# A delta-rule kernel: 64x64 inverse products held as diagonal 32x32 blocks, per-token norms and a moved store

## The chip, the cores and the metric

One core of one Trainium2 chip runs the whole program as a single launch. The metric is device time in microseconds (us). TensorE does the matmuls, VectorE, ScalarE and GpSimd the elementwise work, and the queue of SyncE issues the transfers between HBM and SBUF; products arrive in PSUM.

## What is computed

The program is one layer of a hybrid decoder on 2,048 prompt tokens and 8 groups of 8 sample tokens: a norm and a projection, a state-space half and an RWKV-7 half side by side, an output projection, a convolutional FFN and an embedding gate. The change touches the RWKV-7 half alone. For each of 8 heads of width 64 the reference runs, token by token:

```python
kk = kk / jnp.maximum(jnp.sqrt(jnp.sum(kk * kk, axis=-1, keepdims=True)), L2_EPS)
...
def step(S, inp):
    r_t, w_t, k_t, v_t, kk_t, a_t = inp
    sa = jnp.einsum('bhvk,bhk->bhv', S, -kk_t)
    S = (S * w_t[:, :, None, :] + sa[..., None] * (kk_t * a_t)[:, :, None, :]
         + v_t[..., None] * k_t[:, :, None, :])
    return S, jnp.einsum('bhvk,bhk->bhv', S, r_t)
...
mu = jnp.mean(y, axis=-1, keepdims=True)
var = jnp.mean(jnp.square(y - mu), axis=-1, keepdims=True)
y = ((y - mu) * lax.rsqrt(var + GN_EPS)).reshape(bsz, seq_len, D_RWKV) * lnx_g + lnx_b
bonus = jnp.sum(r4 * k4 * r_k, axis=-1, keepdims=True) * v4
y = (y + bonus.reshape(bsz, seq_len, D_RWKV)) * g
```

There are two norms in it: the length of kk per token and head, and the spread of y per token and head. All arithmetic is fp32.

## The kernel before

The RWKV half is the function delta_rule (L1002). It takes the prompt in 16 turns of 128 tokens (t = 0 to 15) and the 64 sample tokens as a last one. Channels lie on the partitions, two heads of 64 to a column group, four such groups j side by side on the free axis. A turn has two halves, q = 0 and 1, of 64 tokens: a chunk. Within a chunk the recurrence is written as matrices: scores between the chunk's tokens, the inverse of a unit triangular 64x64 matrix for each head, and then the state. The inverse is built in steps: the 16x16 diagonal parts by squaring (D2, D4, D8 and the sums X2, X3, X4), then the off-diagonal parts of 32 (Z32, X32t, X32), then of 64 (Z64, X64t).

The order of a half is written out by hand. STAGES (L986) names 26 products; the first 22 (INTRA) belong to the chunk itself, and the last four (RH, U, S, Y) apply the state for the chunk before and are slotted in behind stages 1, 4, 6 and 8 (STATE_AT, L1070). TensorE walks this list in order (half, L1770), and product (L1659) writes one stage: eight calls, four j by two heads, each a 64x64 stationary matrix and 64 moving columns. One fp32 call shows as two matmul instructions and two weight loads, so a product is 16 and 16. The result goes to one of three PSUM banks of that q in turn, so stage i waits until stage i-3 has been copied out.

VectorE (copy_out, L1341) copies the stages in ADD, most with a mask or an add, and ScalarE (L1528) the stages in PLAIN. One copy is 128x256. In the same in-order queues stand, at stage numbers given by NEXT, BEFORE and HATS (L1411 to L1414 on VectorE, L1552 on ScalarE, L1767 on TensorE), three other kinds of work: prepare makes the next turn's inputs (the low-rank products w and g, ss and bonus; the tanh, exp and square-root steps; the norm nrm, of which VectorE takes a maximum, L1293, and four reciprocals, L1297), hats scales them for a chunk (L1335 to L1339), and finish makes the output rows of the turn before (mean and variance by products with a block matrix, L1765 and L1750, four reciprocals at L1389, then dn, dg, db, dbonus and y, L1392 to L1407). Both norms are held as 128x512: every channel of a head carries its own copy.

GpSimd (turn, L1229) makes the token shift of the next turn: parts low and k first, once the bonus step of the turn before is done on VectorE and the rows Z have landed, then r and v. SyncE's loop runs over t:

```python
for t in range(1, NB):
    if t >= 3:
        store_rows(sp, t - 3)
    sp.wait_ge(prep_pool, at(t - 1, PREP_POOL, "z_v"))
    sp.dma_start(Zp[:], src[:, :, t * TB - 1:(t + 1) * TB]).then_inc(z_in, 16)
```

The store waits for the y step of turn t-3 on VectorE; the load of Z (L1139, 903 KB) stands behind it in the queue. VectorE, ScalarE and GpSimd run the middle turns as a loop, TensorE's turns are written out one after another.

## Time and profile before

| | us |
|---|---|
| median of 3 runs | 3874.78 (3873.79 to 3876.77) |
| the profiled execution, its own time | 3872.04 |
| its span in the trace | 3870.2 |
| projection and state space, before delta_rule | 0 to 985 |
| delta_rule: first turn's preparation | 985 to 1019.5 |
| delta_rule: 16 turns | 1019.5 to 1765 |
| delta_rule: samples and last rows | 1765 to 1846 |
| output projection, FFN, embedding | 1846 to 3870 |

Over the whole span TensorE is busy 3426.3 us (89%) with 32052 matmul instructions and as many weight loads, VectorE 2149.5 (56%), ScalarE 1110.9 (29%) and GpSimd 430.1 (11%). In the profile PE is TensorE, PEld its weight loads, DVE is VectorE, ACT is ScalarE, POOL is GpSimd and SPq is SyncE's queue. A row such as "PE rw_bank<-rw_aT,rw_bT 64*64 64x64 f32 x16" is 16 matmul instructions of a stationary 64x64 and a moving 64x64; the duration of one matmul instruction includes its way through the array, so the spacing of starts, not the duration, tells what a stream costs. Several tiles share a buffer before the change, and the name in a row is that of the buffer: rw_D is also Z, and rw_Dt also D8. The matrices that the trace calls rw_Xt are the inverse under construction.

### The profile page before, as it was taken

What the parts mean: (1) busy time and instruction counts of PE and PEld (TensorE: products, weight loads), DVE (VectorE), ACT (ScalarE), POOL (GpSimd) and SP (SyncE); (2) the same over time, 40 slices, a digit from 0 to 9 for tenths busy, and PEclk for the clock granted to TensorE, in tenths of its full rate; (3) what the DMA queues carried; (4) which work ended last, traced back from release to release, by engine and by line L of the source; (5) the groups of instructions that cost most, each with busy time, mean ns of one, the idle gap of its engine ahead of it and who ended that gap; (6) DMA issues with size and microseconds to landing.
All of it is one profiled execution on the core that took longest, in us unless ns stands there. A gap on an engine that the chain in (4) does not pass through costs nothing.

```text
span 3870.2 us, 75287 instructions
## 1 busy us (share of the span) xinstructions
PE 3426.3 (89%) x32052; PEld 3066.9 (79%) x32052; DVE 2149.5 (56%) x3866; ACT 1110.9 (29%) x2151; POOL 430.1 (11%) x427
## 2 busy tenths in 40 slices
PE   7999974089588888887699999999999999999998
PEld 4666653065477777777699999999999999999998
DVE  2111137951577777774465555666555566665565
ACT  1001021001344444442332222452222245222224
POOL 0000000000333333330300100120000021000001
PEclk9999996569799999997899999999999999999999
DMA  5010011000211111110532222432332243232223
GB/s 200 27 39 26 26 45 13 0 2 31 62 27 27 27 27 27 27 23 22 177 112 70 66 70 66 139 115 77 105 103 68 71 139 105 70 97 75 71 75 114
DMA packets 371660, 257.65 MB, mean 67 GB/s; under 512 B 29584, under 2 KB 361872, under 8 KB 371344
## 3 DMA queue, kind: packets, MB, share of 16 engines
q1 hardware_dynamic: 371360, 253.17, 21.5%
q8 instruction: 247, 4.05, 0.4%
q14 instruction: 53, 0.43, 0.0%
HBM read 217.92 MB, written 34.03 MB: 65 GB/s over the span
## 4 chain that ended last, share of the span: by engine, by line
PE 46%; DVE 3%; ACT 1%; issue 1%; DMA 1%; POOL 0%; SPq 0%; POOLq 0%; DVEq 0%; ACTq 0%
PE oe_pg L892 13%; PE oe_pd L920 13%; PE oe_pv L892 13%; PE oe_pg L953 3%; PE oe_pd L940 3%; DVE oe_w_lo L702 1%; PE oe_pv L960 1%; ACT oe_w_hi L553 0%; DVE oe_rms L733 0%; DMA oe_raw<-in_w_ple 0%; DVE oe_x L718 0%; POOL oe_ys_lo L501 0%; DMA oe_raw<-in_w_out 0%; POOL oe_acc L519 0%; PE oe_pn L881 0%
## 5 line engine op out<-in xcount | busy, mean ns | idle before, releaser
L244 PE MATMUL in_pp<-in_xn,in_w 128*128 (+1 forms) x1728 | 514.3, 460 | 3.7 <-DVE in_xn L200 3.7
L244 PEld LDWEIGHTS in_pp<-in_xn,in_w 128*128 128x128 f32 x1728 | 329.3, 191 | 188.3 <-issue 5.9
L702 DVE TENSOR_TENSOR oe_w_lo<-oe_raw,oe_w_hi 128x1024 fp32r<-128x1024 f32 (+1 forms) x294 | 379.3, 1300 | 112.1 <-ACT oe_w_hi L553 86.7
L709 DVE TENSOR_TENSOR oe_h<-oe_pd,oe_h 128x352 f32<-128x352 f32 x576 | 292.2, 521 | 193.2 <-PE oe_pd L920 140.3
L920 PE MATMUL oe_pd<-oe_f_hi,oe_w_hi 128*128 128x352 f32 x1056 | 342.7, 325 | 8.1 <-DVE oe_h L709 8.1
L892 PE MATMUL oe_pg<-oe_xs_hi,oe_w_hi 128*128 128x352 f32 x1056 | 342.0, 324 | 6.5 <-DVE oe_xs_lo L723 6.5
L920 PE MATMUL oe_pd<-oe_f_hi,oe_w_lo 128*128 128x352 f32 x1056 | 340.4, 322 | 0.0
L920 PE MATMUL oe_pd<-oe_f_lo,oe_w_hi 128*128 128x352 f32 x1056 | 340.4, 322 | 0.0
L892 PE MATMUL oe_pg<-oe_xs_lo,oe_w_hi 128*128 128x352 f32 x1056 | 340.3, 322 | 0.0
L892 PE MATMUL oe_pg<-oe_xs_hi,oe_w_lo 128*128 128x352 f32 x1056 | 340.1, 322 | 0.0
L892 PE MATMUL oe_pv<-oe_xs_lo,oe_w_hi 128*128 128x352 f32 x1056 | 339.8, 322 | 0.0
L892 PE MATMUL oe_pv<-oe_xs_hi,oe_w_hi 128*128 128x352 f32 x1056 | 339.7, 322 | 0.0
L892 PE MATMUL oe_pv<-oe_xs_hi,oe_w_lo 128*128 128x352 f32 x1056 | 339.6, 322 | 0.0
L553 ACT CAST oe_w_hi<-oe_raw 128x1024 fp32r<-128x1024 f32 (+1 forms) x294 | 312.2, 1073 | 89.2 <-DMA oe_raw<-in_w_out 36.6
L619 ACT COPY oe_gp<-oe_pg 128x352 f32<-128x352 f32 x110 | 50.0, 455 | 781.5 <-PE oe_pg L892 781.5
L772 DVE TENSOR_SCALAR oe_cv<-oe_gp,oe_cw 128x352 f32<-128x352 f32 (+1 forms) x132 | 60.3, 457 | 316.1 <-issue 167.9
L920 PEld LDWEIGHTS oe_pd<-oe_f_hi,oe_w_hi 128*128 128x128 f32 x1056 | 199.0, 188 | 12.2 <-DVE oe_h L709 9.6
L892 PEld LDWEIGHTS oe_pg<-oe_xs_hi,oe_w_hi 128*128 128x128 f32 x1056 | 198.7, 188 | 9.4 <-issue 5.5
L151 DVE COPY in_zout<-in_pp 128x352 f32<-128x352 f32 x42 | 22.0, 524 | 322.2 <-PE in_pp L244 322.2
L892 PEld LDWEIGHTS oe_pg<-oe_xs_lo,oe_w_hi 128*128 128x128 f32 x1056 | 198.9, 188 | 0.2
L920 PEld LDWEIGHTS oe_pd<-oe_f_hi,oe_w_lo 128*128 128x128 f32 x1056 | 199.0, 188 | 0.0
L892 PEld LDWEIGHTS oe_pg<-oe_xs_hi,oe_w_lo 128*128 128x128 f32 x1056 | 198.9, 188 | 0.0
(419 smaller groups left out, 7186.2 us busy)
## 6 DMA issues: line engine op xcount, KB each, us to landing
oe_raw<-in_w_gate SPq DMA_DIRECT2D x66, 512.0 KB, 4.0
oe_raw<-in_w_val SPq DMA_DIRECT2D x66, 512.0 KB, 4.0
oe_raw<-in_w_down SPq DMA_DIRECT2D x66, 512.0 KB, 3.6
oe_raw<-in_w_out SPq DMA_DIRECT2D x48, 512.0 KB, 3.7
oe_raw<-in_w_pg SPq DMA_DIRECT2D x48, 512.0 KB, 3.7
scratch_zr<-in_zout SPq DMA_DIRECT2D x12, 1232.0 KB, 4.7
rw_Z<-scratch_zr SPq DMA_DIRECT2D x15, 903.0 KB, 5.8
in_w<-in_w_in SPq DMA_DIRECT2D x6, 1536.0 KB, 16.1
```

What stands on the lines that cost most here:

```text
L151: eng.tensor_copy(dst, src).then_inc(out_sem, 1)
L244: mm = pe.matmul(pp[m % back][:, 0:TW], w[:, k, m * P:(m + 1) * P], xn[:, k, cols(n)], start=(k == 0), stop=(k == KD - 1))
L553: act.copy(w_view(kind, w[i % SLOTS][0]), w_view(kind, raw[i % 2])).then_inc(w_hi, 1)
L619: act.copy(gp[:, 2 + n * TW:2 + (n + 1) * TW], pg[b][:, 0:TW]).then_inc(gate_out, 1)
L702: dve.tensor_tensor(w_view(kind, lo), w_view(kind, raw[i % 2]), w_view(kind, hi).bitcast(F32), ALU.subtract).then_inc(w_lo, 1)
L709: dve.tensor_tensor(hm, pd[sums[key] % 3][:, 0:TW], hm, ALU.add).then_inc(h_ready, 1)
L772: end = dve.tensor_scalar(out, row(2), tap[2], tap[3], ALU.mult, ALU.add)
L892: mm = pe.matmul(out[:, 0:TW], l, r, start=(k == 0 and j == 0), stop=(k == KD - 1 and j == 2))
L920: mm = pe.matmul(pd[turn % 3][:, 0:TW], l, r, start=(q == 0 and j == 0), stop=(q == G - 1 and j == 2))
L940: mm = pe.matmul(pd[turn % 3][:, 0:TW], l, r, start=(k == 0 and j == 0), stop=(k == KD - 1 and j == 2))
L953: mm = pe.matmul(pg[m % 2][:, 0:TW], l, r, start=(k == 0 and j == 0), stop=(k == KD - 1 and j == 2))
L960: mm = pe.matmul(pv[m % 2][:, 0:TW], l, r, start=(k == 0 and j == 0), stop=(k == KP - 1 and j == 2))
```

## The change

Five things are changed, all in delta_rule.

1. The matrices of the inverse are kept as their diagonal 32x32 blocks, 128x128 in all instead of 128x256, and their products (IN_BLOCKS) are written by blocks and scores: four calls for each j, 32 columns each, one for each group of 32 partitions, so 32 instructions and 32 weight loads a product. D2 also computes the off-diagonal block of the scores (O64) in a second half of its bank, in alternation with its blocks for each j, and one ScalarE copy takes both out. X64t multiplies the blocks by 64 columns (E) and ScalarE, no longer VectorE, copies the result (XF). O64's masked copy on VectorE is gone.
2. The two norms are held by token: a sum for each head (per_head_sums) gives 128 tokens x 8, the square root, maximum and reciprocal are taken on that, and two new steps on TensorE (spread) put the values back onto 64 channels each. The eight reciprocals of 128x128 in a turn become two of 128x8.
3. The positions of several steps in the hand-written order are moved (NEXT, BEFORE).
4. SyncE stores the rows of turn t-4 instead of t-3 ahead of the load of Z.
5. At the start, two copies fill a constant part of E, and six matmuls write every PSUM bank once.

```diff
+R = C // 2
+ROWS = [slice(g * R, (g + 1) * R) for g in range(P // R)]
...
+DVE_OUT = ["Dt", "Xt", "D", "O32", "AqbT", "AakT", "X2", "X3", "X4", "X32t", "X32", "AqkT", "Sadd", "S"]
+ACT_OUT = ["D2", "Dt2", "D4", "Dt4", "D8", "Bt", "Kt", "X", "Z32", "Vt", "Z64", "XF", "RH", "U", "Y"]
+COPIED = {"AabT": ["Dt"], "Aab": ["O32"], "X64t": ["XF"], "S": ["Sadd"]}
+IN_BLOCKS = ["AabT", "Aab", "D2", "Dt2", "D4", "Dt4", "X2", "D8", "X3", "X4", "X", "Z32", "X32t", "X32", "Z64"]
...
+        for q, m in enumerate(M):
+            m["D2_O64"] = e.sb(f"D2_O64{q}", [P, 2, HP, R])
+            m["D2"], m["O64"] = m["D2_O64"][:, 0], m["D2_O64"][:, 1]
...
+        def spread(pe, out, per_head, W):
+
+            eye = masks[:, MASKS["eye"]]
+            for j in range(HP):
+                for n, h in enumerate(HALF):
+                    one = per_head[0:W, 2 * j + n:2 * j + n + 1].to_broadcast([W, HD])
+                    last = pe.matmul(v3(out, W)[h, j, :], one, eye[0:W, 0:W], start=True, stop=True)
+            return last
+
+        def per_head_sums(pe, out, rows, ones_, W):
+
+            for j in range(HP):
+                last = pe.matmul(out[0:W, 2 * j:2 * j + 2], v3(rows, W)[:, j, :], ones_, start=True, stop=True)
+            return last
...
                 for t in range(1, NB):
-                    if t >= 3:
-                        store_rows(sp, t - 3)
+                    if t >= 4:
+                        store_rows(sp, t - 4)
                     sp.wait_ge(prep_pool, at(t - 1, PREP_POOL, "z_v"))
...
+                for m in M:
+                    dve.tensor_copy(m["E"][:, :, 0:R], mask("lead")).then_inc(setup, 1)
...
-                        elif step == "nmax":
+                        elif step == "inv":
                             act_did("nrm")
-                            dve.tensor_scalar(b["nrm"], b["nrm"], L2_EPS, None, ALU.max).then_inc(prep_dve, 1)
-                        elif step in range(HP):
-
+                            dve.tensor_scalar(norm[0:W], norm[0:W], L2_EPS, None, ALU.max).then_inc(prep_dve, 1)
                             mine("nmax")
-                            dve.reciprocal(b["nrm"][:, step], b["nrm"][:, step]).then_inc(prep_dve, 1)
+                            dve.reciprocal(norm[0:W], norm[0:W]).then_inc(prep_dve, 1)
...
-                            mine("inv3")
-                            dve.tensor_tensor(b["kkn"], b["kk"], b["nrm"], ALU.mult).then_inc(prep_dve, 1)
+                            dve.wait_ge(prep_pe, at(s, PREP_PE, "spread"))
+                            dve.tensor_tensor(b["kkn"], b["kk"], v3(side[1], W), ALU.mult).then_inc(prep_dve, 1)
...
                     elif stage == "Aab":
-                        masked("D", SD if smp else MD)
-                        masked("O32", NONE if smp else MO32)
-                        masked("O64", NONE if smp else MO64)
+                        masked("D", "low8" if smp else "low16")
+                        masked("O32", "none" if smp else "cross16")
...
-                        masked(stage, SSU if smp else MSU)
-                    elif stage in ("X2", "X3", "X4", "X32t", "X64t"):
+                        masked(stage, "before8" if smp else "before")
+                    elif stage in ("X2", "X3", "X4", "X32t"):
...
-                            dve.reciprocal(sd[:, step], sd[:, step]).then_inc(post_dve, 1)
+                            dve.reciprocal(dev[0:W], dev[0:W]).then_inc(post_dve, 1)
                         elif step == "dn":
-                            mine("inv3")
-                            dve.tensor_tensor(d, d, sd, ALU.mult).then_inc(post_dve, 1)
+                            dve.wait_ge(post_pe, 3 * t + 3)
+                            dve.tensor_tensor(d, d, v3(side[0], W), ALU.mult).then_inc(post_dve, 1)
...
-                ADD = {"AabT", "Aab", "AqbT", "AakT", "X2", "AqkT", "X3", "X4", "X32t", "X32", "X64t"}
-
-                NEXT = [{3: ["kk"], 9: ["L", "t"], 15: ["nmax", 0], 16: [1], 19: ["aa", "sg"]},
-                        {3: [2, 3], 4: ["kkn", "Lp"], 7: ["b", "kp"], 19: ["bonus"]}]
-                BEFORE = [{11: ["d"]}, {8: [0, 1, 2, 3], 11: ["dn"], 13: ["dg", "db"], 14: ["dbonus", "y"]}]
+                ADD = {"AabT", "Aab", "AqbT", "AakT", "X2", "AqkT", "X3", "X4", "X32t", "X32"}
+
+                NEXT = [{3: ["kk"], 9: ["L", "t"], 12: ["inv"], 19: ["aa", "sg"]},
+                        {4: ["kkn", "Lp"], 7: ["b", "kp"], 19: ["bonus"]}]
+                BEFORE = [{13: ["d"], 19: ["inv"]}, {2: ["dn"], 13: ["dg", "db"], 14: ["dbonus", "y"]}]
                 HATS = [{13: ["bT", "aT"], 14: ["kT"]}, {15: ["bT", "aT"], 16: ["kT"]}]
-                REST = [step for i in BEFORE[1] for step in BEFORE[1][i]]
+                REST = ["dn", "dg", "db", "dbonus", "y"]
...
-                            act.activation(b["nrm"], v3(side[1], W), ACT.Sqrt).then_inc(prep_act, 1)
+                            act.activation(norm[0:W], side[1][0:W, 0:2 * HP], ACT.Sqrt).then_inc(prep_act, 1)
...
+                    elif stage == "D2":
+                        src = banks[q][at_][:, 0:2 * HP * R].rearrange("p (a j t) -> p a j t", a=2, t=R)
+                        act.copy(M[q]["D2_O64"][:], src).then_inc(act_out[q], 1)
+                    else:
+                        dst = M[q]["XF"][:] if stage == "X64t" else M[q]["E"][:, :, R:C] if stage == "Z64" else M[q][stage][:]
+                        act.copy(dst, (small if stage in IN_BLOCKS else bank)[q][at_]).then_inc(act_out[q], 1)
...
-                BEFORE = [{12: 0, 16: 1}, {}]
+                BEFORE = [{14: 0, 18: 1}, {}]
...
+                def blocks(out, l, r, j):
+
+                    for g in ROWS:
+                        last = pe.matmul(out[g, j, :], l[g, j, :], ident32[g] if r is None else r[g, j, :], start=True, stop=True)
+                    return last
+
+                def scores(out, rows, cols, j):
+
+                    for n, h in enumerate(HALF):
+                        for i in range(2):
+                            c = slice(i * R, (i + 1) * R)
+                            last = pe.matmul(out[ROWS[2 * n + i], j, :], rows[h, j, c], cols[h, j, c], start=True, stop=True)
                     return last
...
-                            pe.matmul(side[1][:, 0:HP * W], heads(), B["kk2"][:, 0:HP * W], start=True, stop=True).then_inc(prep_pe, 1)
+                            per_head_sums(pe, side[1], B["kk2"], heads()[:, 0:P:HD], W).then_inc(prep_pe, 1)
+                        elif step == "spread":
+                            dve_did("inv")
+                            if not (is_first(s) or s == 1):
+                                pe.wait_ge(post_dve, at(s - 2, POST_DVE, "d"))
+                            spread(pe, side[1], norm, W).then_inc(prep_pe, 1)
...
+                    out = (small if stage in IN_BLOCKS else bank)[q][i % NBANK]
                     for j in range(HP):
-                        for n, (l, r) in enumerate(operands):
-                            last = turned(out, l, j) if transpose else both(out, l, r, j, n == 0, n == len(operands) - 1)
+                        if stage in ("AabT", "Aab"):
+                            (l, r), = operands
+                            last = scores(out, l, r, j)
+                        elif stage == "D2":
+                            (l, r), = operands
+                            a, b = M[q]["aT"], M[q]["bT"]
+                            blocks(out, l, r, j)
+                            for n, h in enumerate(HALF):
+                                last = pe.matmul(corner[q][i % NBANK][ROWS[2 * n + 1], j, :], a[h, j, R:C], b[h, j, 0:R], start=True, stop=True)
+                        elif stage == "Z64":
+                            (l, r), = operands
+                            for n in range(2):
+                                g, g1 = ROWS[2 * n], ROWS[2 * n + 1]
+                                pe.matmul(out[g, j, :], l[g1, j, :], r[g1, j, :], start=True, stop=True)
+                                last = pe.matmul(out[g1, j, :], ident32[g1], ident32[g1], start=True, stop=True)
+                        elif stage in IN_BLOCKS or stage == "X64t":
+                            (l, r), = operands
+                            last = blocks(out, l, r, j)
+                        else:
+                            for n, (l, r) in enumerate(operands):
+                                last = turned(out, l, j) if transpose else both(out, l, r, j, n == 0, n == len(operands) - 1)
...
+                    if part == 2:
+                        pe.wait_ge(post_dve, at(t, POST_DVE, "inv"))
+                        spread(pe, side[0], dev, W).then_inc(post_pe, 1)
+                        return
...
-                        pe.matmul(side[0][:, 0:HP * W], bd64[:], ysq[:, 0:HP * W], start=True, stop=True).then_inc(post_pe, 1)
+                        per_head_sums(pe, side[0], ysq, bd64[:, 0:P:HD], W).then_inc(post_pe, 1)
...
-                NEXT = [{6: ["w"], 8: ["ss"]}, {3: ["g"], 17: ["bonus"]}]
-                BEFORE = [{11: 0, 14: 1}, {}]
+                NEXT = [{6: ["w"], 8: ["ss"], 20: ["spread"]}, {5: ["g"], 17: ["bonus"]}]
+                BEFORE = [{11: 0, 16: 1, 21: 2}, {}]
...
-                prepare(FIRST, "w", "ss", "g", "bonus")
+                for b in banks[0] + banks[1]:
+                    pe.matmul(b[:, 0:HP * C], heads(), S[0][:].rearrange("p j t -> p (j t)"), start=True, stop=True)
+                prepare(FIRST, "w", "ss", "spread", "g", "bonus")
```

## Rows read from the trace of the kernel before

**Rows 1.** All turns: us, busy (instructions) PE, PEld, DVE, ACT, POOL, clock, DMA, GB/s

```profile
1019.50:1765.00 745.50, 631.21 (x15648) 554.61 (x15650) 551.35 (x1020) 332.15 (x836) 246.96 (x258) 0.93 0.11 26
```

**Rows 2.** The same view of one turn, 1247.7 to 1294.9 us

```profile
1247.70:1294.90 47.20, 38.76 (x999) 33.77 (x997) 35.35 (x66) 21.18 (x53) 15.64 (x16) 0.97 0.10 28
```

**Rows 3.** Waits, 1019.5 to 1765 us: waiter, releaser, total us, times, longest

```profile
PE rw_bank L1606 <- DVE rw_Xt L1363: 72.6, 33, 3.8
...
PE rw_bank L1606 <- DVE rw_AakT L1348: 16.0, 12, 2.0
...
PE rw_side L1643 <- ACT rw_p_a L1481: 12.2, 13, 2.1
```

**Rows 4.** Order of time, VectorE: start, us, line, operation, count, [idle before]

```profile
1260.92 0.69 DVE L1277 TENSOR_TENSOR rw_p_kk<-rw_z,rw_k_k 128x512 f32<-128x512 f32 x1 [6.18 <-POOL rw_z L1198]
...
1274.00 1.76 DVE L1297 RECIPROCAL rw_p_kk<-rw_p_kk 128x128 f32<-128x128 f32 x2
...
1287.44 3.38 DVE L1389 RECIPROCAL rw_ysq<-rw_ysq 128x128 f32<-128x128 f32 x4
...
1291.88 0.42 DVE L1363 TENSOR_TENSOR rw_Xt<-rw_bank,rw_Xt 128x256 f32<-128x256 f32 x1 [0.19 <-PE rw_bank L1606]
...
1295.76 0.42 DVE L1339 TENSOR_TENSOR rw_kT<-rw_p_kp,rw_p_E 128x256 f32<-128x256 f32 x1
```

**Rows 5.** Order of time, SyncE's queue: the two loads of Z, a turn apart

```profile
1248.42 0.51 SPq L1139 DMA_DIRECT2D rw_Z<-scratch_zr  x1
...
1295.61 0.51 SPq L1139 DMA_DIRECT2D rw_Z<-scratch_zr  x1
```

**Rows 6.** Order of time, GpSimd: first and last token-shift step of a turn

```profile
1255.50 0.61 POOL L1194 TENSOR_TENSOR rw_z<-rw_Z 128x256 f32<-128x256 f32 x1 [12.25 <-DMA rw_Z<-scratch_zr]
...
1273.77 1.24 POOL L1198 TENSOR_TENSOR rw_z<-rw_z,rw_Z 128x512 f32<-128x512 f32 x1
```

**Rows 7.** Order of time, TensorE: products of 64x64, then one of another shape

```profile
1276.10 0.68 PE L1606 MATMUL rw_bank<-rw_Xt,rw_O 64*64 64x64 f32 x16 [2.32 <-DVE rw_Xt L1363]
...
1277.83 0.66 PE L1606 MATMUL rw_bank<-rw_aT,rw_bT 64*64 64x64 f32 x16
1278.30 0.66 PE L1606 MATMUL rw_bank<-rw_bT,rw_aT 64*64 64x64 f32 x16
...
1280.16 0.66 PE L1606 MATMUL rw_bank<-rw_D,rw_Dt 64*64 64x64 f32 x16
1280.76 1.16 PE L1620 MATMUL rw_side<-rw_p_sx,rw_g 128*128 128x128 f32 x8
```

**Rows 8.** Order of time, TensorE: instructions in two parts of its rows

```profile
1259.01 0.27 PE L1637 MATMUL rw_side<-rw_p_th,rw_w 64*128 64x128 f32 x1
1259.02 0.27 PE L1638 MATMUL rw_side<-rw_z,rw_w 64*128 64x128 f32 x1
1259.12 0.27 PE L1637 MATMUL rw_side<-rw_p_th,rw_w 64*128 64x128 f32 x1
```

**Rows 9.** Order of time, TensorE: instructions in two parts of its columns

```profile
638.96 0.63 PE L2233 MATMUL ss_bk<-ss_U,ss_RTr 128*64 128x264 f32 x4
639.41 0.63 PE L2233 MATMUL ss_bk<-ss_U,ss_RTi 128*64 128x264 f32 x4
```

**Rows 10.** Order of time, ScalarE: the exponentials, and the copy behind them

```profile
1285.76 1.28 ACT L1494 ACT_TABLE_LOAD   x1
...
1288.63 0.62 ACT L1532 COPY rw_Dt<-rw_bank 128x256 f32<-128x256 f32 x2
```

**Rows 11.** Order of time, TensorE: a gap inside the D2 product

```profile
1255.63 0.27 PE L1606 MATMUL rw_bank<-rw_D,rw_Dt 64*64 64x64 f32 x2 [0.98 <-issue]
```

**Rows 12.** Page, third part: queue, kind: packets, MB, share of 16 engines

```profile
q8 instruction: 247, 4.05, 0.4%
```

**Rows 13.** As rows 1: a stretch before the clock falls, and after

```profile
1241.30:1244.70 3.40, 0.97 (x33) 0.84 (x30) 3.21 (x6) 0.77 (x3) 1.87 (x3) 1.00 0.02 5
1244.70:1248.10 3.40, 3.40 (x69) 3.40 (x66) 3.20 (x6) 1.17 (x4) 0.00 (x0) 0.50 0.00 0
```

More of the change, by code:

```diff
@@ L988 @@
 INTRA = STAGES[:22]
-DVE_OUT = ["Dt", "Xt", "D", "O32", "O64", "AqbT", "AakT", "X2", "X3", "X4", "X32t", "X32", "AqkT", "X64t", "Sadd", "S"]
-ACT_OUT = ["D2", "Dt2", "D4", "Dt4", "D8", "Bt", "Kt", "X", "Z32", "Vt", "Z64", "RH", "U", "Y"]
-COPIED = {"AabT": "Dt", "Aab": "O64", "S": "Sadd"}
+DVE_OUT = ["Dt", "Xt", "D", "O32", "AqbT", "AakT", "X2", "X3", "X4", "X32t", "X32", "AqkT", "Sadd", "S"]
+ACT_OUT = ["D2", "Dt2", "D4", "Dt4", "D8", "Bt", "Kt", "X", "Z32", "Vt", "Z64", "XF", "RH", "U", "Y"]
+COPIED = {"AabT": ["Dt"], "Aab": ["O32"], "X64t": ["XF"], "S": ["Sadd"]}
+IN_BLOCKS = ["AabT", "Aab", "D2", "Dt2", "D4", "Dt4", "X2", "D8", "X3", "X4", "X", "Z32", "X32t", "X32", "Z64"]
 HAT_DVE = ["b", "a", "k"]
-POST_DVE = ["d", "inv0", "inv1", "inv2", "inv3", "dn", "dg", "db", "dbonus", "y"]
+POST_DVE = ["d", "inv", "dn", "dg", "db", "dbonus", "y"]
 NBANK = 3
@@ L1343, in copy_out @@
                     m, smp = M[q], is_samples(t)
[L1344 removed]
+                    src = (small if stage in IN_BLOCKS else bank)[q][STAGES.index(stage) % NBANK]
                     dve.wait_ge(mm[q], at(t, STAGES, stage))
@@ L1528, in copy_out @@
                 def copy_out(q, t, stage):
-                    dst = {"Z32": "Z", "Z64": "Z"}.get(stage, stage)
                     act.wait_ge(mm[q], at(t, STAGES, stage))
-                    act.copy(M[q][dst][:], bank[q][STAGES.index(stage) % NBANK]).then_inc(act_out[q], 1)
+                    at_ = STAGES.index(stage) % NBANK
+                    if stage == "D2" and is_samples(t):
+                        act.activation(M[q]["O64"], corner[q][at_], ACT.Copy, scale=0.0)
+                        act.copy(M[q]["D2"], small[q][at_]).then_inc(act_out[q], 1)
+                    elif stage == "D2":
[4 more added lines that the diff above has]
+                        act.copy(dst, (small if stage in IN_BLOCKS else bank)[q][at_]).then_inc(act_out[q], 1)
                 def rows_out(q, t):
@@ L1662, in product @@
                     i = STAGES.index(stage)
-                    names = [copied(n) for n in after] + ([copied(STAGES[i - NBANK])] if i >= NBANK else [])
+                    names = [c for n in [*after, *([STAGES[i - NBANK]] if i >= NBANK else [])] for c in copied(n)]
                     for sem, order in ((dve_out[q], DVE_OUT), (act_out[q], ACT_OUT)):
@@ L1687, in intra @@
                     elif stage == "D2":
-                        product(q, t, stage, [(m["Dt"], m["D"])], after=["Dt", "D"])
+                        product(q, t, stage, [(m["Dt"], m["D"])], after=["AabT", "D"])
                     elif stage == "Dt2":
@@ L1725, in intra @@
                     elif stage == "X64t":
-                        product(q, t, stage, [(m["X"], m["Z"])], after=["X32", "Z64"])
+                        product(q, t, stage, [(m["X"], m["E"])], after=["X32", "Z64"])
                 def with_state(q, t, stage):
@@ L1737, in with_state @@
                     elif stage == "U":
-                        product(q, t, stage, [(m["Xt"], m["RH"])], after=["X64t", "RH"])
+                        product(q, t, stage, [(m["XF"], m["RH"])], after=["X64t", "RH"])
                     elif stage == "S":
@@ L1813, in _ @@
                 for j in range(HP):
-                    last = both(bank[1][2], m["Xt"], m["Z"], j, True, True)
+                    last = both(bank[1][2], m["XF"], M[1]["RH"], j, True, True)
                 last.then_inc(smp_pe, 1)
@@ L1834, in _, with put @@
                 finish(SAMPLES, 1)
+                finish(SAMPLES, 2)
 def rwkv_masks():
     import numpy as np
[L1840 to L1848 removed]
+    i = np.arange(P)[:, None]
+    out = np.zeros((P, MASK_COLS), np.float32)
+    def put(name, chosen, block):
+        t = np.arange(MASKS[name].stop - MASKS[name].start)[None, :]
+        out[:, MASKS[name]] = chosen(i % block, t)
+    put("heads", lambda s, t: s // HD == t // HD, P)
+    put("eye", lambda s, t: s == t, P)
+    put("eye64", lambda s, t: s == t, C)
+    put("before", lambda s, t: s < t, C)
+    put("upto", lambda s, t: s <= t, C)
+    put("before8", lambda s, t: (s < t) & (s // DS == t // DS), C)
+    put("upto8", lambda s, t: (s <= t) & (s // DS == t // DS), C)
+    put("eye32", lambda s, t: s == t, R)
+    put("lead", lambda s, t: s == t, C)
+    put("low16", lambda s, t: (s > t) & (s // 16 == t // 16), R)
+    put("low16_t", lambda s, t: (s < t) & (s // 16 == t // 16), R)
+    put("cross16", lambda s, t: s // 16 > t // 16, R)
+    put("low8", lambda s, t: (s > t) & (s // DS == t // DS), R)
+    put("low8_t", lambda s, t: (s < t) & (s // DS == t // DS), R)
+    return out
 def sample_rows():
```

113 lines of the change are left out of this document (54 added, 59 removed).

## The prediction

> **What bounds the kernel now.** I read the busy time by stretch first: which engine fills the stage that the change touches? In the 745.5 us of the 16 turns TensorE is busy 631.21, VectorE 551.35, ScalarE 332.15 [rows 1]. None is full. A turn lasts 47.2 us, seen from one load of Z to the next [rows 5]; in one such turn TensorE is busy 38.76, VectorE 35.35 [rows 2]. So I asked next for whom TensorE waits. Over all turns it stands 72.6 us for VectorE's adds into the inverse (L1363), 16.0 for VectorE's AakT mask and 12.2 for ScalarE's tanh ahead of ss [rows 3]: 4.5, 1.0 and 0.8 us a turn. The order of time on VectorE says why the adds are late. A maximum over 128x512 and two reciprocals (1.76 us together) stand ahead of the X32t add, and TensorE's Z64 starts after 2.32 us of idling at 1276.10; four more reciprocals (3.38 us) stand ahead of the X3 add [rows 4, 7]. The AakT mask is late because VectorE idles 6.18 us for kk, which needs GpSimd's shift, which waited 12.25 us for the rows of Z [rows 4, 6]. GpSimd had read the old rows for the last time at 1273.77 + 1.24 = 1275.0, but the next load was issued only at 1295.61, behind a store that waits for y [rows 5, 6]. A turn is thus TensorE's own work plus waits for late elementwise work. The clock joins in: after a stretch in which TensorE was busy 0.97 of 3.40 us the granted clock was 0.50, and it was 1.00 before [rows 13]; that is 1.2 instead of 2.4 GHz.
>
> **TensorE's own work before.** Two 64x64 products in a row start 0.47 us apart, 16 instructions each [rows 7]: 0.029 us an instruction. The state's stages RH, S and Y count double, double and triple, so a half is 30 products, 14.0 us, and a turn 28.0. The six side products (w, ss, g, bonus, mean, variance) stream about 0.86 each: eight 128-column instructions at 0.11 [rows 8], or the same number of columns in two wide ones. That is 5.2. A change of the array's shape costs: after a 64x64 product the g product starts 0.60 later instead of 0.47 [rows 7], so 0.13; by the spacing of single instructions I take 0.10. With two changes for each of the six that is 1.2, and 0.4 for weight loads that lie bare behind them. Sum 34.8 us; 47.2 - 34.8 = 12.4 us are waits and the lower clock.
>
> **The blocks.** 24 plain block products in a turn (12 stages, two halves) go from 16 instructions of 64 columns to 32 of 32. The trace of before has no 32-row part. Its nearest rows: instructions in two parts of the rows start 0.01 us apart and each part repeats every 0.11 for 128 columns [rows 8], and two parts of the columns do the same: four instructions of 264 columns in 0.45 us [rows 9]. So parts run side by side, and a part's time goes with its columns, as 0.058 for 64 does. A block product is then eight rounds of four, each half of 0.058 plus a little, 0.032: 0.25 us. That is the low end; the high end is no parallelism at all, 32 x 0.029 = 0.93. I take 0.25, since both rows show full overlap. 24 x (0.25 - 0.47) = -5.3. The four score products save the same, -0.9. X64t stays. D2 becomes blocks and corners, 0.25 + 0.25: no change. The change of shape now comes often: 32-row stages alternate with 64-row ones, and within D2 the shape changes seven times. I count 31 changes in half 0 and 28 in half 1 against 12 a turn before: 47 x 0.10 = +4.7, the low end being 0 (where TensorE waits anyway) and the high 0.13 each, 6.1. Bare weight loads behind them: +0.9.
>
> The rows show 0.10 to 0.13 lost at a change of shape [rows 7]. The Trainium skill says under TensorEngine Tiling (Array Packing), Key Properties, that changing the tiling mode drains TensorE, and the trace agrees; without that rule the 47 changes would be free and the forecast 3741.
>
> **The norms.** ss and the variance become eight instructions with two moving columns; their 128x128 weights still load, and I take what g costs, 0.11 each: +0.1 for both. Two spreads are new, 16 instructions of 128 columns in two column parts, at 8 x 0.11 [rows 8, 9] +0.9 each, or 1.8 if the parts queue: +1.8. TensorE's own work is then 34.8 - 5.3 - 0.9 + 4.7 + 0.9 + 0.1 + 1.8 = 36.1 us. It does not shrink: the gain must come from the waits. New waits: spread waits for VectorE's reciprocal and stands in TensorE's queue ahead of X64t, but that reciprocal is due eight stages earlier; the second spread waits for one that is one short step behind the X32 add, ahead of the next half's scores. Both I take at nothing; the cover is AqkT and X64t, 0.9 us, and without it the cost is about that.
>
> **VectorE and the other queues.** Eight reciprocals (3.52 + 3.38) and the maximum of 1.26 go; two O64 masks and two X64t adds go; sixteen copies or more shrink to half. VectorE loses some 12 of its 35 us, ScalarE stays near 21. So VectorE leaves the path except in one place: from the X4 add to the X32t add it still carries dg, db, dbonus, y and three hats, 1291.88 to 1296.18 [rows 4]. TensorE has X, Z32, Vt, X32t, bonus and X32 to do meanwhile, some 2.9 us; 1.4 us of waiting stay in half 1. Half 0 has d and the hats there: 1.5. On ScalarE the exponentials with their table load take 1285.76 to 1288.63 [rows 10] ahead of the D8 copy: about 0.7 of waiting for X4. ss still waits for two sets of tanh: 0.8.
>
> **The store.** The load of Z can be issued at 1275.0 instead of 1295.6, so GpSimd starts at bonus, some 4 us before 1255.50. VectorE waits about 2 us for kk instead of 6.18, and AakT's mask no longer holds TensorE: -1.0. The store itself is an earlier turn's and has long been due; behind it only the load is queued. If the load still came late, the 1.0 would stay.
>
> **Instructions.** TensorE's instructions of all turns are fetched: 247 packets [rows 12] for 64,000 matmuls and loads, one for about 260. Inside D2 TensorE idled 0.98 us for nothing the profile names [rows 11], just while the load of 1248.42 ran. A turn before has 1,980 of them, after 3,160. I take 1.5 us a turn, between 0.5 (about as now) and 4.
>
> **The sum.** 36.1 + 1.4 + 1.5 + 0.7 + 0.8 + 1.5 (fetch) + 1.3 (clock) + 0.4 (small ones) = 43.7 us a turn. 16.5 turns x 3.5 = -58. Ahead of the first turn six matmuls of 256 columns cost 2.9 us at the full clock, 5.8 at half; the first preparation and the last rows lose reciprocals, about 3: net +2. 3872 - 58 + 2 = 3816 for an execution like the profiled one, whose 3872.04 is 2.7 below the median: 3818.
>
> **The rivals.**
> *TensorE does not pack the blocks.* If four parts cannot be fed at once, a block product costs more than 0.25. The 28 of them break the gain even at 0.25 + 3.5/28 = 0.38 us. At 0.47 a turn is 49.8: 3918. At 0.93 it is 62.7: about 4130. For it: only two parts are ever seen at once. Against: their 0.01 us between starts leaves room for four in 0.032. Chance 0.17.
> The Trainium skill, in the same page under Instruction Overhead, gives each matmul some 60 cycles however few columns it has and warns against tiling a dimension that is already small. That is this rival in its middle: by that page an estimate is 32 x 0.025 = 0.80 us, a turn of 59, 4073. Two starts 0.01 apart [rows 8] speak against it, unless the floor holds in each part.
> *Fetching binds.* With 60% more instructions and a burst of 64 in each block product, the gap of rows 11 comes at each fetch that meets the load of Z: 3 to 4 us a turn, 46: 3856. Chance 0.14.
> *The clock.* Small parts and gaps leave TensorE at 0.50 for long; if a third of its work ran so, +12 us a turn, about 4010. Against: its waits shrink. Chance 0.06.
> *Changes of shape are hidden* behind waits, or VectorE is out of the way entirely: 39 to 41 us, 3740 to 3775. Chance 0.15.
> *Nothing moves,* since TensorE's work is as long as before and other waits take the place of the old: 3867 to 3882. Chance 0.08.
>
> **How the numbers follow.** The forecast has 0.40, with a range of its own of 3790 to 3850. About 0.2% is what a measurement of this kernel can tell from no change, 7.7 us. Faster: 0.40 + 0.15 + most of the fetch case = 0.68. Same 0.08. Slower: 0.17 + 0.06 and a little = 0.24. The range takes in the hidden changes at its low end and packing at 0.45 us a product at its high end, 3740 to 3910; outside remain the worse halves of two rivals.
>
> **What would show it.** Right: block products starting 0.25 to 0.29 apart in a row and some 0.36 before a change of shape; no reciprocal over 0.2 us on VectorE; the load of Z issued right behind GpSimd's last shift step; TensorE's waits for L1363's successor down to about 3 us a turn; a turn of 43 to 44. Wrong: four blocks starting 0.03 apart each, a granted clock under 0.9 over the turns, or gaps inside products at each load of Z.

## The result, and the profile after

The changed kernel takes 3954.61 us (median of 4 runs, 3950.19 to 3967.77); the kernel before took 3874.28 beside it. The ratio is 1.021, 95% interval 1.0187 to 1.0237: 80 us slower, where 3818 was forecast with a range of 3740 to 3910. The profiled execution took 3956.61 us, its span is 3954.8. Of the four runs of the second experiment below, one is left out: it took 4163 us at a granted clock of 0.81, the other three 3926 to 3938 us.

The page's busy times first (busy, share of the span, instructions), then its row on the instruction queue (packets, MB, share of 16 engines):

```profile
PE 3496.6 (88%) x41788; PEld 3111.5 (79%) x41788; DVE 1987.6 (50%) x3700; ACT 1088.7 (28%) x2185; POOL 436.4 (11%) x427
...
q8 instruction: 323, 5.29, 0.6%
```

The instructions of all engines came in 247 packets before [rows 12], 323 now. Next a steady stretch of 500 us inside the turns (us, busy of PE, PEld, DVE, ACT, POOL, granted clock, DMA share, GB/s):

```profile
1100.00:1600.00 500.00, 421.96 (x15408) 359.63 (x15412) 249.25 (x534) 194.69 (x540) 157.27 (x156) 0.91 0.10 26
```

By VectorE's last step of y, ten turns around this stretch take 51.75 us each; before it was 47.4. VectorE is busy half the time now, 0.74 of it before [rows 1]: the reciprocals are gone, and many of its copies are half as long. For whom does TensorE wait instead? The waits of the same stretch (waiter, releaser, total us, times, longest):

```profile
PE rw_side L1127 <- ACT rw_ysq L1578: 25.2, 9, 3.0
PE rw_bank L1650 <- issue: 23.7, 26, 1.6
PE rw_bank L1639 <- issue: 10.9, 16, 1.5
PE rw_bank L1658 <- issue: 5.1, 5, 1.6
PE rw_side L1127 <- ACT rw_p_a L1506: 4.0, 8, 0.6
PE rw_bank L1644 <- issue: 3.3, 3, 1.4
PE rw_bank L1730 <- issue: 2.9, 5, 0.8
```

The waits for VectorE's adds and the AakT mask, 72.6 and 16.0 us over the turns before [rows 3], have left the list. Two kinds took their place. The first row is the variance's sum of squares (L1127); it waits for ScalarE's square, 2.6 us a turn. And all lines with "issue" together, three small ones included that are not shown, make 48.0 us, 5.0 a turn: TensorE stands still and the profile names no releaser. Before, such waits came to 4.5 us in as long a stretch.

Where the second kind sits, TensorE shows in order of time, inside D2 (start, us, line, tiles, shape, count, [idle before]):

```profile
1323.63 0.26 PE L1650 MATMUL rw_bank<-rw_D,rw_Dt 32*32 32x32 f32 x8
1323.83 0.25 PE L1730 MATMUL rw_bank<-rw_bT,rw_aT 64*32 64x32 f32 x4
1324.01 0.26 PE L1650 MATMUL rw_bank<-rw_D,rw_Dt 32*32 32x32 f32 x8
1324.20 0.21 PE L1730 MATMUL rw_bank<-rw_bT,rw_aT 64*32 64x32 f32 x1
1325.06 0.25 PE L1730 MATMUL rw_bank<-rw_bT,rw_aT 64*32 64x32 f32 x3 [0.64 <-issue]
...
1330.09 0.45 PE L1650 MATMUL rw_bank<-rw_Dt,rw_D_O 32*32 32x32 f32 x32
1330.37 0.48 PE L1650 MATMUL rw_bank<-rw_Xt,rw_D_O 32*32 32x32 f32 x32
1330.77 0.33 PE L1639 MATMUL rw_bank<-rw_rT,rw_S 64*64 64x64 f32 x4
```

One matmul of a product whose operands are all there starts at 1324.20, the other three of its four 0.86 us later. The DMA view of 1322 to 1326 us (40 slices of 0.1 us) shows what went on meanwhile:

```profile
GB/s 0 0 0 0 0 0 0 164 0 0 0 0 0 0 0 0 0 0 0 0 0 0 0 0 0 0 0 0 0 0 0 0 0 0 0 0 0 0 0 0
...
q8 instruction: 1, 0.02, 1.5%
```

A single packet, of instructions, starting at 1322.7; TensorE goes on 2.3 us behind it. No load of Z runs here. I summed, over 1020 to 1765 us, all steps of more than 0.33 us between two starts inside a product: 83.6 us in 82 places, and in 79 of them TensorE resumes 2.1 to 3.0 us after a packet's start. Before it was 7.8 us in 8 places, all 8 with the same delay. Those 8 and these 82 differ in what the packet had met: before, 7 of the packets started while a load of Z was in flight, 6.2 to 11.6 us behind the packet ahead of them; now 2 of 82 did, and half of the 82 came within 3.8 us of the packet ahead. There are 178 packets in that stretch, half of them less than 3.86 us apart and none less than 3.25. Between 1020 and 1830 us TensorE starts 48,906 matmuls and weight loads while 192 packets come in: 255 for each.

The other wait. VectorE, ScalarE and TensorE in order of time in half 0 of a turn:

```profile
1286.18 0.29 DVE L1388 TENSOR_TENSOR rw_Xt<-rw_bank,rw_Xt 128x128 f32<-128x128 f32 x1 [2.48 <-PE rw_bank L1650]
...
1287.08 0.20 DVE L1323 RECIPROCAL rw_norm<-rw_norm 128x8 f32<-128x8 f32 x1
1287.20 1.10 DVE L1361 TENSOR_TENSOR rw_bT<-rw_p_b,rw_p_E 128x256 f32<-128x256 f32 x1
1288.22 1.25 DVE L1363 SCALAR_TENSOR_TENSOR rw_aT<-rw_p_kkn,rw_p_Lp 128x256 f32<-128x256 f32 x1
1289.40 0.67 DVE L1411 TENSOR_TENSOR rw_yt<-rw_yt,rw_side 128x512 f32<-128x512 f32 x1
```

```profile
1290.10 0.63 ACT L1578 ACTIVATE rw_ysq<-rw_yt 128x512 f32<-128x512 f32 x1 [2.41 <-DVE rw_yt L1411]
```

```profile
1287.58 0.68 PE L1644 MATMUL rw_bank<-rw_masks,rw_vT 64*64 64x64 f32 x16
1290.79 1.86 PE L1127 MATMUL rw_side<-rw_bd,rw_ysq 128*128 128x2 f32 x8 [2.53 <-ACT rw_ysq L1578]
```

VectorE's d (L1411) now stands behind the hats bT and aT, which take 1.10 and 1.25 us, and ScalarE's square waits for d. The TensorE rows behind the wait are slow as well. Two stretches (columns as above) show it: TensorE is busy 0.87 of 3.40 us, and then the granted clock is 0.50, the lower level, as in [rows 13]:

```profile
1287.60:1291.00 3.40, 0.87 (x21) 0.73 (x18) 3.19 (x4) 0.99 (x4) 2.75 (x3) 0.86 0.02 5
1291.00:1294.40 3.40, 3.40 (x108) 3.20 (x109) 0.87 (x4) 0.46 (x3) 0.00 (x0) 0.50 0.78 218
```

And one turn near the end is 65.8 us long. VectorE's y there, and SyncE's queue:

```profile
1797.12 0.69 DVE L1432 TENSOR_TENSOR rw_yb<-rw_yt,rw_g_h 128x512 f32<-128x512 f32 x1 [12.53 <-DMA scratch_y<-rw_yb]
```

```profile
1783.29 10.92 SPq L1169 DMA_DIRECT2D rw_Z<-scratch_zr  x14
1794.25 3.95 SPq L1145 DMA_DIRECT2D scratch_y<-rw_yb  x2
```

y of a turn may be written once the turn before is stored. That store, NB-4's, was issued inside the loop before. Now it stands behind the 14 loads of the sample rows, and those wait for the last turn's token shift.

### The profile page after: what moved, and what is told of

Read it like the earlier page. It is cut to its first block, busy times and chain, and to the rows that moved or that the text cites. A ratio compares the mean times of both kernels' runs of the same rounds, so it can differ in the third digit from the quotient of the medians.

```text
span 3954.8 us, 94582 instructions
## 1 busy us (share of the span) xinstructions
PE 3496.6 (88%) x41788; PEld 3111.5 (79%) x41788; DVE 1987.6 (50%) x3700; ACT 1088.7 (28%) x2185; POOL 436.4 (11%) x427
## 3 DMA queue, kind: packets, MB, share of 16 engines
q8 instruction: 323, 5.29, 0.6%
## 4 chain that ended last, share of the span: by engine, by line
PE 46%; DVE 2%; ACT 1%; issue 1%; POOL 0%; SPq 0%; DMA 0%; POOLq 0%; DVEq 0%; ACTq 0%
PE oe_pg L892 13%; PE oe_pd L920 12%; PE oe_pv L892 12%; PE oe_pg L953 4%; PE oe_pd L940 4%; PE oe_pv L960 1%; DVE oe_w_lo L702 1%; DVE oe_rms L733 0%; DVE oe_x L718 0%; POOL oe_ys_lo L501 0%; PE oe_pn L881 0%; ACT oe_w_hi L553 0%; POOL oe_acc L519 0%; DMA oe_st<-in_state_conv 0%; DVE oe_h L709 0%
## 5 line engine op out<-in xcount | busy, mean ns | idle before, releaser
L892 PEld LDWEIGHTS oe_pv<-oe_xs_hi,oe_w_lo 128*128 128x128 f32 x1056 | 198.5, 188 | 0.0
```

Of the source, the lines that this page charges most:

```text
L892: mm = pe.matmul(out[:, 0:TW], l, r, start=(k == 0 and j == 0), stop=(k == KD - 1 and j == 2))
```

## The experiments

The theory: TensorE's instructions arrive too slowly for the blocks (5 us a turn), the late square adds 2.6 and the low clock behind it, and the store's new place costs some 12 us once. The rivals: the blocks' own streaming, the changes of shape, the norms' new work, or the store itself. Each result below is the median time, with its ratio to the kernel before run beside it and the 95% interval of that ratio; "the 500 us" is the stretch from 1100 to 1600 us.

**Without the blocks.** The kernel before with norms, order and store of the change:

```diff
 # kernel before, plus:
+ spread(...), per_head_sums(...)          # norms by token, as in the change
- NEXT = ... 15: ["nmax", 0], 16: [1] ... 3: [2, 3]
+ NEXT = ... 12: ["inv"] ...
- if t >= 3: store_rows(sp, t - 3)
+ if t >= 4: store_rows(sp, t - 4)
```

> The kernel before with the norms by token, the new order on the queues and the later store, but with every product of the inverse still in 64x64 parts. If the blocks' extra instructions are what lost the time (theory: TensorE waits for its instructions, some 5 us a turn), a turn has 2,000 instructions again, the gaps inside products go back to about 0.5 us a turn and the time falls below the kernel before: a turn of 44 to 45.5 us, 3820 to 3850 us, although the variance still waits 2.7 us for its square. If norms, order or store lost it, this kernel is slower than before as well: 3890 us or more.

This kernel took 3848.3 us, ratio 0.993 [0.991, 0.995]. A turn takes 45.1 us, and in the 500 us there is no wait for "issue" at all; the variance still waits 28.7 us. The blocks turn a gain into a loss.

**d ahead of the hats**, in the changed kernel:

```diff
- BEFORE = [{13: ["d"], 19: ["inv"]}, ...
+ BEFORE = [{12: ["d"], 19: ["inv"]}, ...
```

> The changed kernel with one step moved: VectorE subtracts the mean (d) after stage 12 of half 0, ahead of the hats bT and aT, instead of after stage 13 behind them. If the late square holds TensorE (theory: 2.75 to 3.2 us at the variance, once a turn, and the low clock after it), the wait falls below 0.5 us and the time by 40 to 60 us, to 3895 to 3915. If the hats that now come 0.7 us later are awaited just as long, or another step is late next, the time stays within 10 us of 3955.

It took 3928.2 us (three runs), ratio 1.015 [1.013, 1.017]: 26 us won where 40 to 60 were expected. The wait for the square fell from 25.2 to 2.4 us in the 500, so that was its cause. A turn fell from 51.75 to 49.65 us, nearly by the wait itself (2.4 us a turn). The waits for instructions stayed at 5.0 us a turn (50.2 us against 48.0), and the granted clock stayed at 0.91: the low clock that the expectation counted with the wait did not go with it.

**The store alone**, in the kernel before:

```diff
- if t >= 3: store_rows(sp, t - 3)
+ if t >= 4: store_rows(sp, t - 4)
```

> The kernel before with the store of y moved alone (four turns behind instead of three). My forecast's term: 1.0 us a turn gained, 3858 us, with VectorE's wait for kk down from 6.2 to about 2 us and the load of Z issued right behind GpSimd's last shift step. Rival: GpSimd's shift now falls beside VectorE's hats and both run slower (1.1 instead of 0.42 us each), so that nothing is won or up to 1 us a turn is lost: 3870 to 3890.

It took 3844.9 us, ratio 0.992 [0.991, 0.994]: 29 us won, more than my term. A turn falls from 47.4 to 44.9 us, and TensorE's wait for the AakT mask [rows 3] is gone from the list. The hats of half 0 were as slow in the kernel before, so the rival had no new cost to bring (see "A wait that was not listed"). One turn of 55.0 us at the end gives some back.

**Half the instructions in 24 block products**, in the changed kernel:

```diff
- for g in ROWS:
-     pe.matmul(out[g, j, :], l[g, j, :], r[g, j, :], ...)
+ if j % 2:
+     for g in ROWS:
+         pe.matmul(out[g, j - 1:j + 1, :], l[g, j, :], r[g, j - 1:j + 1, :], ...)
```

> The changed kernel with half the instructions in 24 block products a turn: each 32x32 weight block is multiplied with the 64 moving columns of two neighbouring head pairs, so the columns streamed, the shape changes, the copies and the order stay as they are, and 768 of some 3,160 TensorE instructions a turn are gone. (The product of one head of each pair is then computed with its neighbour's weights.) If instructions not yet fetched stop TensorE (theory), the gaps inside products fall from 5 to about 2 us a turn and the time by 40 to 60 us, to 3895 to 3915. If the time went to the blocks' own streaming, the shape changes or the variance, it stays within 12 us of 3955.

It took 3869.6 us, ratio 0.999 [0.998, 1.000]: 85 us less than the changed kernel, more than expected. The waits for instructions fall from 48.0 to 2.9 us in the 500. The main cause is the instructions. One thing did not stay as the expectation says: D2's blocks now stand at every second j alone, so its shape changes four times inside, not seven. How much of the 85 us this and the halved products' own streaming make is worked out further down.

**The mends.** The first mend is d ahead of the hats, as above. The second puts the store of turn NB-4 ahead of the samples' loads:

```diff
+ store_rows(sp, NB - 4)
  sp.wait_ge(prep_pool, at(NB - 1, PREP_POOL, "z_v"))
  ...
- store_rows(sp, NB - 4)
  store_rows(sp, NB - 3)
```

> The first experiment's kernel (norms by token and the later store, 64x64 products) with two mends: VectorE's d after stage 12, ahead of the hats, and the store of turn NB-4 issued ahead of the 14 loads of the samples instead of behind them. Theory: the variance's wait (38 us over the turns there) all but goes, and the one long turn at the end (55.5 instead of 45 us, y waiting for that store) is a normal one: 3848 - 33 - 10 = 3805, between 3795 and 3820. Rival: the time that d frees is lost to the hats that come later, and only the 10 us of the tail are won: 3835 to 3842.

It took 3797.9 us, ratio 0.980 [0.978, 0.982]: faster than both kernels. A turn takes 42.1 us. Its 500 us and its waits:

```profile
1100.00:1600.00 500.00, 470.59 (x12301) 426.24 (x12298) 338.23 (x698) 241.64 (x627) 201.07 (x191) 0.99 0.11 31
```

```profile
PE rw_bank L1621 <- DVE rw_Xt L1378: 11.0, 23, 0.6
PE rw_side L1118 <- ACT rw_p_a L1496: 8.1, 12, 0.7
PE rw_bank L1621 <- ACT rw_Dt L1547: 5.9, 12, 0.5
PE rw_side L1118 <- ACT rw_ysq L1560: 1.2, 8, 0.2
PE rw_bank L1621 <- issue: 0.2, 1, 0.2
```

No wait is longer than 0.7 us, and the granted clock is 0.99 where the kernel before had 0.94.

The store with the second mend, without the norms:

> The kernel before with the store moved and the store of turn NB-4 ahead of the samples' loads, nothing else. Theory: y of one turn no longer waits 9.8 us for the store behind those loads: 3845 - 10 = 3835, between 3830 and 3840. If that turn is long for another reason, 3843 to 3847.

It took 3841.4 us, ratio 0.992 [0.990, 0.994]: the long turn is 45.3 instead of 55.0 us, as expected, but the time fell by 3.5 us, not 10; the next turn is 2.1 us longer, and turns of one kernel differ by up to 2 us. The place of the loss is shown, its size in this kernel is not.

Both mends on the changed kernel:

> The changed kernel, blocks and all, with the same two mends (d early, store of NB-4 ahead of the samples' loads). Theory: 3933 (with d early alone) less 10 to 14 for the tail: 3917 to 3925, still slower than before, because TensorE's instructions come in at some 3.8 us for 256 and a turn needs over 12 such packets. Against the same kernel with 64x64 products this gives the blocks' own cost: about 115 us, 7 us a turn. If the blocks were held up by the variance and the tail, not by instructions, it falls below 3875.

It took 3920.3 us, ratio 1.013 [1.011, 1.014], with a turn of 49.9 us and waits for instructions of 52.4 us in the 500. Against 64x64 products in the same frame the blocks cost 122 us.

**ss one stage later.**

```diff
- NEXT = [{6: ["w"], 8: ["ss"], 20: ["spread"]}, ...
+ NEXT = [{6: ["w"], 9: ["ss"], 20: ["spread"]}, ...
```

> The kernel of e5_best with one step more: ss (and ScalarE's square root behind it) one stage later in half 0, after stage 9. TensorE waits 0.7 us a turn there for ScalarE's second set of tanh (11.9 us over the turns). Theory: that wait is covered by the D8 product and 5 to 12 us are won over e5_best. Rival: the norm then comes late for VectorE's reciprocal or D8's copy waits behind the square root: within 3 us of e5_best or slower.

It took 3800.4 us, within the spread of the runs of 3797.9: the rival. The wait for the tanh fell from 8.1 to 2.6 us in the 500, but the waits for the square and the norm grew by more, from 1.2 to 6.2 and from none to 3.5.

**What the blocks cost without their instructions.** The mended kernel with half the instructions:

> The changed kernel with the two mends and half the instructions in the 24 block products (one head of each pair computed with its neighbour's weights, same columns, same changes of shape). Against the mended kernel, 3920, it takes away the waits for instructions alone: theory 92 us of gaps in 15 turns down to some 8, so 3920 - 85 to 95 = 3825 to 3840. What is then left above the 64x64 kernel with the same mends, 3798, is the blocks' price without their instructions: 30 to 40 us, 2 us a turn, which the 47 changes of shape would explain. My forecast had the blocks at 0.6 us a turn better than 64x64 before their instructions: 3790. If instructions are not the cause, it stays above 3900.

It took 3836.2 us, ratio 0.990 [0.988, 0.992]: 84 us below the mended kernel, 38 above the 64x64 one. Its 500 us and first waits:

```profile
1100.00:1600.00 500.00, 446.72 (x13544) 372.50 (x13540) 298.00 (x624) 221.43 (x622) 183.33 (x184) 0.92 0.11 30
```

```profile
PE rw_bank L1742 <- DVE rw_Xt L1388: 26.7, 23, 1.6
PE rw_side L1127 <- ACT rw_ysq L1578: 7.8, 11, 0.7
PE rw_side L1127 <- ACT rw_p_a L1506: 7.7, 11, 0.7
```

A turn is 44.4 us, so TensorE is busy 446.72 / (500 / 44.4) = 39.7 us of it; with 64x64 products 470.59 / (500 / 42.1) = 39.6. The 2.3 us by which the turn is longer are idle time, above all the wait of Z64 (L1742) for the X32t add. But equal busy times do not mean equal work, for the clocks differ, 0.92 against 0.99. The clock has two levels in these traces, 1.00 and 0.50; in the 500 us it was at 0.50 for 75 us here and for 14 with 64x64 products. No wait here is longer than 1.6 us, and still the clock falls once a turn (columns as above):

```profile
1299.15:1302.56 3.41, 1.99 (x53) 1.68 (x48) 3.41 (x5) 1.33 (x4) 3.25 (x4) 1.00 0.00 0
1302.56:1309.38 6.82, 6.59 (x123) 5.58 (x127) 1.96 (x6) 0.77 (x3) 1.01 (x1) 0.50 0.49 137
```

In the trace of before, 64x64 products in a row start 0.85 us apart at 0.50 and 0.47 at 1.00, so 0.45 of the time at the lower level is lost. TensorE was busy at it for 6.0 us a turn here and 1.2 with 64x64 products. By an estimate from these numbers the lower level cost 2.7 and 0.5 us a turn: at one clock the halved blocks would be busy some 2.2 us less. The forecast's clock term is taken up again below.

**D2's blocks first, its corners behind them**, with half and with all instructions:

```diff
- for j in range(HP): blocks(out, l, r, j); corners(j)
+ for j in range(HP): blocks(out, l, r, j)
+ for j in range(HP): corners(j)
```

> The kernel before this one in the list, with D2's blocks for all pairs first and its corners behind them, instead of in turns: one change of shape inside the product instead of about seven, twice a turn. With instructions out of the way and 0.06 to 0.1 us a change, D2 falls from about 1.0 to 0.6 us and the time by 0.7 us a turn: 8 to 14 us. If a change inside a product is free, or another wait takes it up, within 3 us.

With half the instructions it took 3825.8 us, 10.4 below: a change of shape inside a product has its price. D2 falls from 1.10 to 0.73 us, counted to the next product's start. In this kernel three changes go, four less one, not six; twice a turn over 16.5 turns that is 0.105 us for each.

> The changed kernel with the two mends and D2's blocks before its corners, all instructions kept and nothing left out. If the instructions' supply sets the pace (theory), what the shape changes give back is mostly eaten by the next wait for instructions: 0 to 8 us below 3920. If the changes of shape are what the blocks lost by, as much as with half the instructions, 8 to 14 us or more.

With all instructions it took 3909.7 us, 10.6 below the mended kernel, but its runs spread from 3894 to 3918, so the time alone doesn't tell the two readings apart. The trace says more: here six changes go, and D2 falls from 1.50 to 0.76 us, 1.5 us a turn. Waits for instructions rose from 52.4 to 63.5 us in the 500, by some 1.0 us a turn, and 10.6 us are 0.6 a turn. Most of what D2 gave back went into the next wait for instructions, as the first reading has it.

**The output steps spread out**, on 64x64 products and on the half-instruction blocks:

```diff
- {2: ["dn"], 13: ["dg", "db"], 14: ["dbonus", "y"]}
+ {2: ["dn"], 5: ["dg", "db"], 10: ["dbonus", "y"]}
```

> The kernel with norms by token, the later store and both mends on 64x64 products (3798), and VectorE's four output steps spread to its idle places of half 1: dg and db after stage 5, dbonus and y after stage 10, instead of all four ahead of the hats and the X32t add. TensorE waits 15.0 us over the turns for the Xt adds there. Theory: half 1's share of it, some 0.6 us a turn, goes: 3785 to 3794. Rival: X3's add, now behind dbonus and y, is late instead: within 4 us of 3798 or slower.

It took 3794.8 us, ratio 0.980 [0.978, 0.982]: 3 below 3797.9, inside the spread of the runs. The granted clock is 1.00 in the 500 us.

> The same move of the four output steps in the blocks' kernel with half the instructions and D2's corners last (3826; one head of each pair computed with its neighbour's weights). TensorE waits 34.3 us over the turns there, ahead of Z64, for the X32t add that stands behind dg, db, dbonus, y and the hats. If that wait and the low clock behind it are what keeps the blocks above the 64x64 kernel once instructions are out of the way, 15 to 25 us are won: 3800 to 3811, the 64x64 kernel's level. If it is the changes of shape, 8 us at most.

It took 3826.8 us: nothing won. The waits ahead of Z64 fell from 26.7 to 8.6 us in the 500, but X2 to X4 now wait 9.2 and the waits for instructions doubled, 9.9 to 19.8:

```profile
PE rw_bank L1654 <- DVE rw_Xt L1388: 9.2, 11, 0.9
PE rw_bank L1750 <- DVE rw_Xt L1388: 8.6, 11, 0.9
PE rw_bank L1639 <- issue: 8.0, 7, 2.1
...
PE rw_bank L1665 <- issue: 6.1, 4, 1.7
...
PE rw_bank L1654 <- issue: 4.6, 5, 1.6
```

So neither of its two readings is shown: the wait was not the bound by itself, nor are shapes shown to be. The low clock behind it was not put to the test, for it stayed: 0.92, or 75 us of the 500 at 0.50, where the 64x64 kernel with the same move has none. By the estimate above that is some 2.9 us a turn, more than the 2.3 between the two turns (44.4 and 42.1). How the last 28 us divide between instructions, these waits, shapes and the clock stays open.

## Why the forecast was wrong

Between runs that differ in one part of the change the 80 us divide thus: store moved and its tail mended -33 (3874 to 3841); norms by token, with the moved steps and d early, -43 (to 3798); blocks +38 (to 3836, instructions halved); their other instructions +84 (to 3920); d behind the hats and the store behind the samples' loads +34 (to 3955). The halved products also free TensorE 0.02 to 0.03 us earlier each, and D2 takes 1.1 instead of 1.5 us, mostly by its three changes of shape less; together that is about 1.3 us a turn, so some 20 of the 84 are not instructions.

**Instructions: the step that failed.** I took 1.5 us a turn, between 0.5 and 4; it was 5.0 by the waits, 5.8 by the steps between starts. I scaled the one gap of [rows 11] and tied it to the load of Z. The rival "fetching binds" did the same and got 3856. For the kernel before that tie was right (7 of its 8 steps), but now the gaps come anywhere in the turn, without a load (2 of 82). The bound stood in the trace of before: no two of its packets start less than 3.32 us apart. A turn of 3,160 instructions needs 12.3 packets, so at least 41 us, and 47 at the 3.86 seen now, against a forecast turn of 43.7. I never set the supply's time beside the turn. Bursts ask for more still: by the spacing of starts, four block products in a row use up a packet in 1.1 us (4 x 0.27), eight 64x64 products in 3.8 (8 x 0.47).

**A wait that was not listed.** I followed d and the hats only to the X32t add behind them on VectorE. d is also awaited by the square, and the square by the variance: 2.6 us a turn, which I had at nothing. The hats stood in my sum at 0.42 us each, as kT in [rows 4]; but that row is of half 1. In half 0 they were slow before the change too, beside GpSimd's shift steps (from 1270.09 us on in that turn):

```profile
1270.21 1.40 DVE L1337 SCALAR_TENSOR_TENSOR rw_aT<-rw_p_kkn,rw_p_Lp 128x256 f32<-128x256 f32 x1
1271.53 1.25 DVE L1339 TENSOR_TENSOR rw_kT<-rw_p_kp,rw_p_E 128x256 f32<-128x256 f32 x1
```

What the change did was to put d behind them.

**The store.** Right in kind: the load of Z is issued at 1290.54, and GpSimd's last step ends at 1289.27 + 1.24. Too small: 2.5 us a turn instead of 1.0, of which 1.4 is idle time of TensorE and 1.2 busy time, at a clock of 0.96 instead of 0.94 in the 500 us. And wrong in "behind it only the load is queued": past the loop it is queued behind 14 loads, and y waits 12.53 us for it, once.

**The blocks themselves.** Right. Two products of four 32x32 parts start 0.27 to 0.28 us apart in a row and 0.38 to 0.40 ahead of another shape (rows of 1330.09 to 1330.77), where 0.25 and 0.36 were forecast; the first rival, packing, fell. A change of shape costs 0.12 us there, 0.10 taken. The Trainium skill's floor of some 60 cycles for each matmul (TensorEngine Tiling (Array Packing), Instruction Overhead) would by an estimate make 32 of them 0.80 us; these rows disagree for TensorE as a whole, though not for a floor in each of the four parts. A spread takes 1.02 us to the next product's start, that product's change of shape included (0.9 and 0.10 forecast). By busy time halved blocks and 64x64 products are equal; at one clock, by the estimate above, the blocks are 2.2 us a turn ahead, of which about 1.3 came with the halving. I had 0.6 in the blocks' favour.

**Norms and VectorE.** Right: with 64x64 products and d early the waits for the Xt adds fall from 55.0 to 11.0 us in the 500, and the norms, the moved steps and d early together are worth 43 us. VectorE's busy time fell from 35.2 to 25.8 us a turn, 9.4 less, where I had some 12. Without its blocks and with the two mends the change gives 3798, 20 us more than the forecast gain; without the mends 3848.

**The clock.** A second term that failed: I put 1.3 us a turn into the sum and gave no row for it. In the 500 us the granted clock was at 0.50 for 92 us, before for 61, and TensorE was busy in nearly all of that, 9.2 and 5.8 us a turn. By the estimate above this cost 4.1 us a turn, before 2.6. The sign that I had named, a granted clock under 0.9 over the turns, came in: 0.88 from 1020 to 1830 us. (The rival's 12 us a turn give 4016, not 4010.) The long wait for the square is not the whole cause: with d early the clock is 0.91 as well, and halved blocks with both mends have 0.92, where 64x64 products in the same frame have 0.99. What in the blocks' order brings it down stays open. Against my sum the three terms come to 3.5 (instructions), 2.6 (the square) and 2.8 us (the clock), where the turn missed its forecast by 8.0; the store's larger gain goes the other way, and the rest is not divided further.

## What to carry to other kernels

Before a product is cut into smaller parts, count instructions for a stretch, divide by those of a packet, and multiply by the shortest distance between two packets in the trace: if that comes near the stretch's time, reckon with the instructions as the bound, whatever the array could do. Before busy times of two kernels are compared, compare their granted clocks. When a step is moved, follow its consumers on other engines to the end of the chain, and the steps of its queue past the loop as well. Of a change in several parts, measure each alone: here two parts were worth 76 us and the third cost more than both.

## What the runs showed of the hardware

TensorE's instructions came in packets of 16 KB (5.29 MB / 323), one for about 255 matmuls and weight loads, in no run less than 3.2 us apart, and where TensorE had stopped inside a product it resumed 2.1 to 3.0 us after a packet's start (79 of 82 places). Four 32x32 parts took a matmul every 8 ns (32 in 0.27 us). A change of the array's shape cost about 0.1 us (0.12 between the products of 1330.09 to 1330.77, 0.105 each by what D2's three fewer changes gave back). VectorE's hats of 128x256 took 1.10 to 1.40 us beside a GpSimd shift step and 0.42 without.
